# The query stage in ten packed jobs of 128 rows per token chunk, in a kernel for a hybrid decoder layer

## What is computed

```python
def mla_queries(q_lat, cos, sin, g_q_lat, w_uq, g_q_nope, g_q_rope):
    cq = rmsnorm(q_lat, g_q_lat)                      # 384 wide
    q = jnp.einsum('blc,chd->blhd', cq, w_uq)         # 8 heads, 64 + 32
    qn = rmsnorm(q[..., :QK_NOPE], g_q_nope)          # per head, 64
    qr = apply_rope(rmsnorm(q[..., QK_NOPE:], g_q_rope), cos[:, None, :], sin[:, None, :])   # per head, 32
    return qn, qr

def mla_keys(ckv, w_uk, g_k_nope):
    return rmsnorm(jnp.einsum('...kc,chd->...khd', ckv, w_uk), g_k_nope)    # ckv 256 wide, per head 64
```

## Time and profile before

| | |
|---|---|
| median of 3 runs | 3681.6 us (3671.5 to 3682.8) |
| span of the profiled execution | 3684.9 us |
| that execution against the median of the runs | 3.3 us more |
| PE, DVE, ACT, POOL busy | 84%, 71%, 37%, 30% |
| DMA queue of the gather | 73.7% of 16 engines over the span |
| front stage, query stage, tail (from the timeline) | 0 to 158, 158 to 350.7, 350.7 to 3684.9 us |

### The profile page before, as it was taken

One profiled execution on the slowest core, in us unless ns is written; L12 is line 12 of the kernel. 1 busy time (PEld: TensorE's weight loads), 2 busy tenths in 40 slices (PEclk: granted clock), 3 DMA queues, 4 the chain that ended last, 5 costly groups with the idle time before them and its releaser, 6 DMA issues.

```text
span 3684.9 us, 34349 instructions
## 1 busy us (share of the span) xinstructions
PE 3113.5 (84%) x9808; PEld 1717.8 (47%) x9808; DVE 2613.8 (71%) x5837; ACT 1363.1 (37%) x3986; POOL 1090.7 (30%) x1252
## 2 busy tenths in 40 slices
PE   7996898868899999677878897899778988878877
PEld 4433686524455555233444443454334545455421
DVE  3264114897777779987677867879987687766864
ACT  2221202348722233255564222244244344422343
POOL 0000001333333333343333333233333343323342
PEclk9997699978899999787889998899888898866999
DMA  2111255999999998899999999999999999989998
GB/s 106 51 38 45 83 154 184 420 383 396 388 412 419 413 383 340 332 388 405 400 409 419 420 417 420 417 406 407 412 394 413 367 415 416 391 349 413 419 421 368
DMA packets 233053, 1274.50 MB, mean 346 GB/s; under 512 B 45019, under 2 KB 62491, under 8 KB 97380
## 3 DMA queue, kind: packets, MB, share of 16 engines
q0 software_dynamic: 152064, 1107.36, 73.7%
q1 hardware_dynamic: 79076, 160.60, 12.5%
q10 hardware_dynamic: 1728, 4.39, 0.3%
HBM read 1258.85 MB, written 13.40 MB: 345 GB/s over the span
## 4 chain that ended last, share of the span: by engine, by line
PE 33%; DMA 22%; DVE 22%; ACT 7%; issue 5%; POOL 1%; SPq 0%; DVEq 0%; POOLq 0%; ACTq 0%
DMA tl_uv<-in_uv,tl_idx 22%; PE tl_y L939 11%; DVE tl_uv L1522 8%; PE tl_f L1194 6%; DVE tl_acc L1503 4%; PE tl_f L1222 3%; PE tl_f L1169 2%; PE tl_f L1205 2%; PE tl_f L1000 2%; PE tl_f L1113 1%; POOL tl_uv L870 1%; PE tl_f L1064 1%; PE tl_f L1136 1%; ACT L1269 1%; ACT tl_att_s L1382 1%
## 5 line engine op out<-in xcount | busy, mean ns | idle before, releaser
L870 POOL DMA_INDIRECT tl_uv<-in_uv,tl_idx x1056 | 1044.4, 989 | 1895.3 <-PE tl_y L939 1170.4
L1522 DVE CUSTOM_DVE_ANT_0 tl_uv<-tl_uv,tl_h 128x1024 f32<-128x1024 f32 x1056 | 1268.2, 1216 | 413.6 <-DMA tl_uv<-in_uv,tl_idx 389.2
L939 PE MATMUL tl_y<-tl_uv,tl_diag 128*128 128x512 f32 (+1 forms) x2460 | 1297.8, 670 | 304.2 <-ACT tl_diag L1241 286.8
L939 PEld LDWEIGHTS tl_y<-tl_uv,tl_diag 128*128 128x128 f32 (+1 forms) x2460 | 484.2, 208 | 962.5 <-issue 499.1
L1269 ACT ACTIVATE tl_ge<-tl_a 128x1 f32<-128x1 f32 x1056 | 210.3, 199 | 1240.5 <-DVE tl_a L1522 1202.6
L1503 DVE SCALAR_TENSOR_TENSOR tl_acc<-tl_uv,tl_w,tl_acc 128x1024 f32<-128x1024 f32 x433 | 555.0, 1282 | 67.2 <-ACT tl_w L1253 66.2
L1253 ACT ACTIVATE tl_w<-tl_ge,tl_weight 128x1 f32<-128x1 f32 x1024 | 301.5, 294 | 33.3
L1222 PE MATMUL tl_f<-H,w_tail 128*128 128x384 f32 (+2 forms) x1024 | 267.4, 417 | 6.4 <-DVE H L1835 6.2
L1241 ACT ACTIVATE tl_diag<-K,tl_w 128x128 f32<-128x128 f32 (+1 forms) x615 | 244.4, 397 | 45.8 <-PE tl_y L939 25.4
L1194 PE MATMUL tl_f<-H,w_tail 128*128 128x256 f32 (+2 forms) x768 | 235.2, 463 | 1.4 <-DVE tl_ya L1803 1.4
L1222 PEld LDWEIGHTS tl_f<-H,w_tail 128*128 128x128 f32 x1024 | 184.2, 200 | 102.3 <-issue 36.0
(11 more groups left out here) (237 smaller groups left out, 3070.3 us busy)
## 6 DMA issues: line engine op xcount, KB each, us to landing
w_tail<-in_w_merge SPq DMA_DIRECT2D x80, 512.0 KB
w_tail<-in_w_peer SPq DMA_DIRECT2D x64, 576.0 KB
w_tail<-in_w_conv SPq DMA_DIRECT2D x36, 512.0 KB
tl_uv<-in_uv,tl_idx POOLq DMA_INDIRECT x1056
w_tail<-in_w_mix SPq DMA_DIRECT2D x32, 512.0 KB
X<-in_cache SPq DMA_DIRECT2D x48, 128.0 KB
X<-in_x SPq DMA_DIRECT2D x8, 536.0 KB, 7.2
o_y<-tl_acc ACTq DMA_DIRECT2D x8, 512.0 KB
```

Of the source, the lines that this page charges most:

```text
L870: pool.indirect_dma_start(UV[:, u % RING, :], None, d["uv"], bass.IndirectOffsetOnAxis(ap=which, axis=0)).then_inc(landed[u % RING], 16)
L939: mm = pe.matmul(Y[0:m, half * 512:(half + 1) * 512], DG[:, (pe_count[u] - 1) % DIAGS, 0:m], UV[:, u % RING, D + half * 512:D + (half + 1) ...
L1522: dve.tensor_tensor_reduce(UV[:, u % RING, 0:D], UV[:, u % RING, 0:D], HP[:], 1.0, 0.0, ALU.mult, ALU.add, A[:, t % 2, i:i + 1]).then_inc( ...
```

## The change

The outer loop of the query stage now runs over the three token chunks (360, 360 and 352 tokens, samples included), the inner one over ten jobs that each fill 128 output rows: 4 key jobs (two heads each), 4 jobs of the queries' nope parts (two heads each), and 2 jobs of the rope parts (four heads each). The weights are packed so on the host and all loaded in the front stage (`HeadWeights`), so nothing is reloaded. A chunk's sums go to 24 rows of one bank, two or four per job. Raw rows are scaled in place in `RAW`, which has two slots of ten jobs; `SQ` has three buffers in rotation. A spread of the chunk before stands behind every job from the third on, the last two behind the last sum. The ropes turn 128 rows at a time, behind the ten scalings of their chunk. SyncE stores a chunk with three DMAs (`s_k`, `s_qn`, `s_qr`). The hardware loop is gone; the code is written out. The absorbed matmuls are the same 16, in two banks; the gain, the copies and the outputs around them are done once, after the last chunk. In the tail a head's queries come with two DMAs, since they lie in two tensors.

The diff, cut to its core; of the removed lines of the engines' code only the functions printed above tell.

```diff
-NJ, ROWS = 6, 9
-C_SUM = C_EPS + 1
-C_ID4 = C_SUM + NJ * ROWS
+NJ, ROWS = 10, 24
+C_SUM2 = C_EPS + 1
+C_SUM4 = C_SUM2 + 22 + ROWS
+C_ID4 = C_SUM4 + 20 + ROWS
...
+class HeadWeights:
+
+
+    PARTS = [0, 4 * KT * P, 4 * KT * P + 6 * QT * P]
+
+    def __init__(self, nc, ctx, d):
+        self.tile = ctx.enter_context(nc.sbuf_tensor("w_head", [P, self.PARTS[-1]], F32))
+        self.arrived = [ctx.enter_context(nc.semaphore(f"w_head_in{s}")) for s in range(2)]
+        self.source = d["w_head"]
+
+    def load(self, sp):
+        for s in range(2):
+            part = slice(self.PARTS[s], self.PARTS[s + 1])
+            sp.dma_start(self.tile[:, part], self.source[:, part]).then_inc(self.arrived[s], 16)
+
+    def block(self, j, k):
+        at = (j * KT + k) * P if j < 4 else self.PARTS[1] + ((j - 4) * QT + k) * P
+        return self.tile[:, at:at + P]
...
-        WUT = sb("wukT", [NOPE, NH, KVL])
-        G = sb("gains", [P, 2])
-        S = sb("spread", [ROWS, NJ * HD])
-        RAW = sb("raw", [HD, 2, NJ, 360])
-        SQ = sb("sq", [HD, NJ, 360])
-        RI = sb("root", [ROWS, 2, 360])
-        Q = sb("q", [HD, 2, TQ])
-        KH = sb("k", [NOPE, 2, T])
-        SW = sb("swap", [HD, 360])
-        QG = sb("qg", [NOPE, NH, NS])
-        PAD = sb("pad", [1, 1])
...
+        WUT = sb("wukT", [P, NH // 2, KVL])
+        G = sb("gains", [P, 3])
+        S = sb("spread", [ROWS, NJ, P])
+        RAW = sb("raw", [P, 2, NJ, CMAX])
+        SQ = sb("sq", [P, 3, CMAX])
+        RI = sb("root", [ROWS, 2, CMAX])
+        SW = sb("swap", [P, 2, CMAX])
+        QG = sb("qg", [P, NH // 2, NS])
         PS = ctx.enter_context(nc.psum_tensor("qr_ps", [P, 8, 512], F32))
...
-        JOBS = [(False, a, n) for a, n in CHUNKS] + [(True, a, n) for a, n in QCH]
-        BEHIND = ((), (), (0,), (1,), (2, 3), (4, 5))
...
+            for c, (a, n) in enumerate(CHUNKS):
+                s, lo, hi = c % 2, max(a, META), min(a + n, KEYS)
+                sp.wait_ge(ready, c + 1)
+                sp.dma_start(d["s_k"].rearrange("(j b) p n -> (b p) j n", b=2)[:, :, a:hi], RAW[:, s, 0:4, 0:hi - a]
+                             ).then_inc(stored[s], 16)
+                sp.dma_start(d["s_qn"].rearrange("(j b) p n -> (b p) j n", b=2)[:, :, lo - META:hi - META],
+                             RAW[:, s, 4:8, lo - a:hi - a]).then_inc(stored[s], 16)
+                sp.dma_start(d["s_qr"].rearrange("(j b) p n -> (b p) j n", b=4)[:, :, lo - META:hi - META],
+                             RAW[:, s, 8:10, lo - a:hi - a]).then_inc(stored[s], 16)
+            sp.wait_ge(asked, 1)
+            sp.dma_start(d["s_qrs"], QRS[:]).then_inc(sample_kept, 16)
+            sp.wait_ge(abs_set, 2 * KT)
+            sp.dma_start(d["s_qabs"], QABS[:]).then_inc(sample_kept, 16)
...
         def _(pe):
+            def sums(c, j):
+                n = CHUNKS[c][1]
+                pe.wait_ge(sq, at(c, j) + 1)
+                if j == 0 and c >= 2:
+                    pe.wait_ge(root, c - 1)
+                first = C_SUM4 + 20 - (16 + 4 * (j - 8)) if j >= 8 else C_SUM2 + 22 - 2 * j
+                pe.matmul(PS[0:ROWS, SUMS + c % 2, 0:n], K[:, first:first + ROWS], SQ[:, at(c, j) % 3, 0:n],
                           start=(j == 0), stop=(j == NJ - 1)).then_inc(ss, 1)
 
+            def back(c, j):
+                n = CHUNKS[c][1]
+                if c == 0 and j == 0:
+                    pe.wait_ge(spread_in, 16)
+                if j == 0:
+                    pe.wait_ge(inv, c + 1)
+                if at(c, j) >= 2:
+                    pe.wait_ge(normed, at(c, j) - 1)
+                pe.matmul(PS[:, SPREAD + at(c, j) % 2, 0:n], S[:, j, :], RI[:, c % 2, 0:n],
+                          start=True, stop=True).then_inc(spread, 1)
+
+            for c, (a, n) in enumerate(CHUNKS):
+                for j in range(NJ):
+                    if c == 0 and j == 0:
+                        pe.wait_ge(weights.arrived[0], 16)
+                    if c == 0 and j == 4:
+                        pe.wait_ge(weights.arrived[1], 16)
+                    if at(c, j) >= 3:
+                        pe.wait_ge(sq, at(c, j) - 2)
+                    nk, x = (KT, CKV) if j < 4 else (QT, CQ)
                     for k in range(nk):
+                        mm = pe.matmul(PS[:, at(c, j) % 3, 0:n], weights.block(j, k), x[:, k, a:a + n],
+                                       start=(k == 0), stop=(k == nk - 1))
                     mm.then_inc(raw, 1)
                     if j:
+                        sums(c, j - 1)
+                    if c and j >= 2:
+                        back(c - 1, j - 2)
+                sums(c, NJ - 1)
+                if c:
+                    back(c - 1, NJ - 2)
+                    back(c - 1, NJ - 1)
+            for j in range(NJ):
+                back(NC - 1, j)
+            pe.wait_ge(asked, 1)
             pe.wait_ge(small_in, 32)
             for h in range(NH):
+                r = slice(h % 2 * NOPE, (h % 2 + 1) * NOPE)
                 for k in range(KT):
+                    mm = pe.matmul(PS[:, ABS[h % 2], (h // 2 * KT + k) * NS:(h // 2 * KT + k + 1) * NS],
+                                   WUT[r, h // 2, k * P:(k + 1) * P], QG[r, h // 2, :], start=True, stop=True,
+                                   skip_group_check=True)
+                mm.then_inc(qabs, 1)
 
         @block.scalar
         def _(act):
+            for c, (a, n) in enumerate(CHUNKS):
+                s = c % 2
+                for j in range(NJ):
+                    act.wait_ge(raw, at(c, j) + 1)
+                    if j == 0 and c >= 2:
+                        act.wait_ge(stored[s], 48 * (c // 2))
+                    act.activation(RAW[:, s, j, 0:n], PS[:, at(c, j) % 3, 0:n], ACT.Copy)
+                    if at(c, j) >= 3:
+                        act.wait_ge(ss, at(c, j) - 2)
+                    act.activation(SQ[:, at(c, j) % 3, 0:n], PS[:, at(c, j) % 3, 0:n], ACT.Square).then_inc(sq, 1)
+                act.wait_ge(ss, at(c + 1, 0))
+                if c >= 2:
+                    act.wait_ge(spread, at(c - 1, 0))
+                act.activation(RI[:, s, 0:n], PS[0:ROWS, SUMS + s, 0:n], ACT.Sqrt, bias=K[0:ROWS, C_EPS:C_EPS + 1]
+                               ).then_inc(root, 1)
 
         @block.vector
         def _(dve):
             dve.wait_ge(small_in, 32)
+            for c, (a, n) in enumerate(CHUNKS):
+                s = c % 2
+                dve.wait_ge(root, c + 1)
+                dve.reciprocal(RI[:, s, 0:n], RI[:, s, 0:n]).then_inc(inv, 1)
+                for j in range(NJ):
+                    g = 0 if j < 4 else 1 if j < 8 else 2
+                    dve.wait_ge(spread, at(c, j) + 1)
+                    dve.scalar_tensor_tensor(RAW[:, s, j, 0:n], RAW[:, s, j, 0:n], G[:, g:g + 1],
+                                             PS[:, SPREAD + at(c, j) % 2, 0:n], ALU.mult, ALU.mult).then_inc(normed, 1)
+                for i in range(2):
+                    q = RAW[:, s, 8 + i, 0:n]
+                    dve.wait_ge(normed, at(c, 8 + i) + 1)
+                    rope(dve, q, q, SW[:, i, 0:n], CS, a, n, step, 4 * (2 * c + i))
+                dve.wait_ge(step, 8 * (c + 1))
+                dve.wait_ge(normed, at(c + 1, 0))
+                dve.sem_inc(ready, 1)
+            own = slice(KEYS - CHUNKS[-1][0], T - CHUNKS[-1][0])
+            s = (NC - 1) % 2
+            dve.tensor_scalar(QG[:], RAW[:, s, 4:8, own], G[:, 0:1], None, ALU.mult).then_inc(step, 1)
+            for h in range(NH):
+                r = slice(h % 4 * ROPE, (h % 4 + 1) * ROPE)
+                dve.tensor_copy(QRS[:, :, h, :], RAW[r, s, 8 + h // 4, own].rearrange("p (s q) -> p s q", q=DSEQ)
+                                ).then_inc(step, 1)
+            dve.wait_ge(step, 8 * NC + 1 + NH)
+            dve.sem_inc(asked, 1)
+            dve.wait_ge(qabs, NH)
+            for b in range(2):
+                for k in range(KT):
+                    dve.tensor_copy(QABS[:, k, :, b::2].rearrange("p s h q -> p h s q"),
+                                    PS[:, ABS[b], 0:NH // 2 * KT * NS].rearrange("p (h k s q) -> p k h s q", k=KT, q=DSEQ, s=NSEQ)[:, k]
+                                    ).then_inc(abs_set, 1)
 
 
...
-                    if c:
-                        sp.dma_start(H[0:HD, s * TMAX:s * TMAX + per, META:META + P],
-                                     d["s_q"][h, :, a:a + n].rearrange("p (t n) -> p t n", n=P)).then_inc(qk_in[s], 16)
-                    else:
-                        sp.dma_start(AQ[:, s, 0:n], d["s_q"][h, :, a:a + n]).then_inc(qk_in[s], 16)
+                    for r, part in ((slice(0, NOPE), d["s_qn"]), (slice(NOPE, HD), d["s_qr"])):
+                        if c:
+                            sp.dma_start(H[r, s * TMAX:s * TMAX + per, META:META + P],
+                                         part[h, :, a:a + n].rearrange("p (t n) -> p t n", n=P)).then_inc(qk_in[s], 16)
+                        else:
```

(28 more changed lines are left out.)

139 lines of the change are left out of this document (24 added, 115 removed).

## The result

| | median of 4 runs | ratio, 95% | span of the profiled execution |
|---|---|---|---|
| before | 3682.2 us (3671.5 to 3687.1) | | 3684.9 us |
| after | 3623.2 us (3617.6 to 3631.5) | 0.9845 [0.9825, 0.9865] | 3621.5 us |

The forecast was 3628 us with a range of 3612 to 3642. The span of the profiled execution fell by 63.4 us, against 53.6 forecast. The next stage's first issue came at 292.0 us instead of 350.7, 58.7 us earlier, where 54.5 had been forecast. The other 4.7 us of the 63.4 came behind it, and lie within what that part varies by from run to run (12 us, see Experiments).

The account below looks back on a forecast made before the run. PE carries the query stage; the DMA-busy gather behind it sets the end. Stage end 350.7 to 296.2 us, 54.5 less; span 3684.9 less 54.5 plus 0.9 is 3631.3, less 3.3 to the median: 3628 us, range 3612 to 3642.

Parts of the forecast that it names:

- Matmuls, 46 us: Query stage on PE: 138 matmuls for the three chunks against 216, 78 x 0.59 = 46 us less.
- edges: Changes between kinds of matmul on PE: 0.14 us each, 20 in the first chunk, 30 in each other.
- Reciprocals: Root and reciprocal, 0.6 + 2.4 us, lie under the next chunk's first three projections, 5 us.
- rest, 2 us: Old kernel, each 20.65 us head: the remaining 2 us is PE waiting for the reciprocal.
- The new wait: Before the third chunk's first sum: PE stands 10.8 us until the first chunk's stores, taken as 7.5 us, free the slot.
- Slow restart, 2.5 us: Third chunk's start: PE at clock 0.50 for 4.9 us after the idle stretch, costing 2.5 us.
- Rival B: Clock does not come back after the new wait; third chunk's 42 matmuls take 24.7 us more: 3650 us, chance 0.06.
- The stage's end: From 260.4 us, hidden by nothing: ropes, reciprocal, ten spreads 11.5, absorbed matmuls 7.0, copies, store, barrier; ends at 296.2 us.
- the absorbed matmuls, 7.0 forecast: Near the query stage's end: the 16 absorbed matmuls take 7.0 us, as in the trace of before.
- Outside: Tail: two query loads per head instead of one make first scores 0.9 us later; front stage's larger weights cost nothing.
- Rivals D: Attention stage's 70 us at clock 0.50 may run at full clock and give back up to 20: 3608 us, chance 0.05.
- E: The gain doesn't arrive because the gather runs slower by as much, 1.8%: 3681 us, chance 0.04.

Follow-up runs that it names:

- scale2: The changed kernel with a copy of each spread put on VectorE ahead of each scaling; next stage's first issue at 299.5 us, 3628.9 us in one run.
- behind: The kernel before, unpacked, with a head's first two spreads both behind the fourth projection; next stage's first issue at 334.6 us, 3668.6 us in one run.
- slot3: The changed kernel with three slots of raw rows instead of two; next stage's first issue at 281.9 us, median 3613.6 us, ratio 0.9818.
- warm: The changed kernel with 15, 11 and 10 unread matmuls before three slow places; next stage's first issue at 287.0 us, 3614.0 us in one run.
- evens: The changed kernel with the absorbed matmuls of even heads first, then odd; these took 6.21 us instead of 3.64, 3620.6 us in one run.
- Halves_alt: The changed kernel with each key and nope projection as two 64-row halves in turn, block by block; next stage's first issue at 291.6 us, 3626.4 us.

## Why the prediction was right, and where it was off

*Matmuls, 46 us; edges.* Right. The interior step of 3.53 us is five matmuls of 0.60, 3.0, and three edges of 0.18, where I took 0.14; over the stage the edges cost some 1.8 us more than counted. The first chunk ended at 182.5 (forecast 184.0), because the stage began 0.5 us earlier and at the full clock, which gave some 1.8 us back. That the two cancel is luck: with the same front stage, scale2 began at the low clock. The last spread of the second chunk ended at 214.9 (215.8).

*Reciprocals.* Right that the waits go, but they were read too large. My "rest, 2 us" of each head was not the reciprocal alone: PE stood up to 1.65 us for it and 0.6 to 0.7 for ScalarE's square. In behind the reciprocal waits alone are gone, and they are worth 10.3 us of the gain, which the old kernel could have had without packing. The forecast of the new stage did not rest on this. The reciprocal of chunk 0 lay under projections as I said; that of chunk 1 began at 219.9, behind VectorE's ropes, and only the stall hid it, as the 2.0 us in slot3 show.

*The new wait.* Right in place, cause and order: ropes, three stores, copy, square, sum. PE stood 9.6 us (10.8 forecast). The stores took 6.4 us from 219.87 to 226.28, not 7.5. The store rate I took, 261 GB/s, was the row of one head's smaller stores; here it was 295 over four us. The Trainium skill, *DMA: Bandwidth & Descriptors*, section Anatomy of one DMA, led to 6.1 as an estimate, and this trace is nearer to it, though the page fits DMAs that GpSimd issues and these are SyncE's.

*Slow restart, 2.5 us.* About 2.1: in warm, where PE was busy in the stall, the way from the first sum behind it to the last spreads took 36.8 us and not 38.9. The clock was 0.54 from 228 to 232 and 1.00 behind that, and the last spread of chunk 1 ended at 258.7 (260.4). Rival B is out.

*The stage's end.* Ropes and reciprocal came as forecast. The spreads with their last scaling took 12.7 us for 11.5, at the low clock throughout: the upper bound, 12.6, was nearly right and my choice below it was not. **The term that was mis-sized is the absorbed matmuls, 7.0 forecast, 3.64 measured.** I carried them over as "the same 16" from the earlier trace rows; but packed by pairs their inputs alternate between the row halves, and their outputs between two banks, and evens shows that the order in turn is worth 2.6 us of the 3.4. The Trainium skill, *TensorE: Matmul & The Clock Gate*, section Packing small matmuls — row/col tiling, says that matmuls which use different rows or columns of the array run at the same time, and that the start partitions of operands and output choose the place; the trace agrees, 3.64 against 6.21 us, as far as it is the halves and not the banks, and I did not apply it. At the last spreads the stage was 1.75 us ahead of the forecast (266.05 against 267.8), spreads and copies took 1.5 of that back (284.88 against 285.1), the absorbed matmuls gave 3.4, the copies and the barrier behind them 0.6: the 4.2 by which the mark came earlier than forecast.

*Outside.* The first score came 5.1 us behind the mark instead of 4.6, so two loads for one cost 0.5 us and not 0.9. Rivals D and E are out: attention at 0.50, the gather at 0.98 and 398 GB/s. The gather's first issue came 61.0 us earlier, its last 64.5; the difference of 3.5 is less than the 12 us by which the time behind the mark varies, and I claim no cause for it. For the same reason the last few us of the median, 3623 for 3628, are no test of the forecast; the mark is.

*A reading that was incomplete.* I put the gain down to fewer matmuls because each job is 128 rows wide. Halves_alt shows that the width as such is not needed: the same job in two halves costs the same if they stand side by side. What the old order paid for in its key jobs was half-wide matmuls that all began at row 0. Its query jobs have 96 rows, of which no two fit side by side in 128, so for them this is no way out.

The sum of the gain, from both traces, first from the stage's first matmul to the last spreads (167.8 us before, 108.5 now): 47.7 for 82 matmuls fewer, 10.3 for the reciprocal waits, 4.1 for the waits for the square, about 4 for edges (what is left over), 3.3 for the clock at 304, 1.3 for the clock at the start; less 11.7 for the seam (9.6 of stall and 2.1 of restart). Then 3.4 for the absorbed matmuls and 0.5 for the earlier start, less 4.5 for the longer end (14.3 us from the last spreads to the absorbed matmuls before, 18.8 now). That makes the 58.7. The 1.8 us at the start can't be credited to the change: behind, with the old front stage, began at 157.0 us and at the full clock.

## What to carry to other kernels

Before giving up a narrow output, see where each matmul's output begins: 64-row matmuls at partitions 0 and 64, in turn, cost as much as one of 128 rows. When a stage is cut into fewer, larger steps, look at the seams: here a last piece of the old chunk stood behind the new one's work, and together with a missing buffer it cost 17 us of the 76 that were to be had. Price a stage's end by itself: there one engine works with nothing beside it, and here the end became 4.5 us longer while the stage had fewer matmuls. Before you compare a mark inside two executions, compare where their stage began and at what clock.
